# The S5 tail and the mLSTM branch of a two-block transformer kernel, put into one program block: the mLSTM in eight half-head units on six PSUM banks, S5's activation, gate and projection beside it

## What is computed

```python
h_ml = mlstm_memory(mq, mk, mv, mi + ml_i_b, mf + ml_f_b)      # 4 heads, keys of 64, values of 128
y_ml = jax.nn.sigmoid(mo) * h_ml.reshape(bsz, t, -1)
y_s5 = jax.nn.gelu(s5_ssm(su, ...))                            # 512 channels
y_s5 = y_s5 * jax.nn.sigmoid(y_s5 @ s5_glu_w + s5_glu_b)
gates = jax.nn.sigmoid(zg + branch_gate_b).reshape(bsz, t, N_BRANCH, D_MODEL)
merged = (gates[:, :, 0] * (y_gla @ proj_gla)
          + gates[:, :, 1] * (y_ml @ proj_ml)
          + gates[:, :, 2] * (y_s5 @ proj_s5))
```

```python
scores = (q @ k.T) * exp(d_intra - m)                # inside the chunk, causal
num = w_inter * (q @ mem) + scores @ v               # mem: the state from the chunks before
den = w_inter * (q @ norm) + sum(scores)
h = num / maximum(abs(den), exp(-m))
```

## Time and profile before

| | |
|---|---|
| median of 3 runs | 3596.35 us (3596.18 to 3603.19) |
| profiled execution, its own time | 3594.54 us |
| its span in the profile | 3592.8 us |
| PE busy | 3126.1 us (87%), 14192 matmuls |
| PEld / DVE / ACT / POOL busy | 2351.6 / 1329.7 / 958.9 / 814.7 us |

### The profile page before, as it was taken

How to read it: one execution, slowest core, us unless ns; L and a number is a source line. 1 busy time by engine, 2 the same in 40 slices (tenths; PEclk the granted TensorE clock), 3 DMA queues, 4 the chain that set the end, 5 groups by cost and what they waited for, 6 DMA issues and landing times. The chain is left out here.

```text
span 3592.8 us, 34192 instructions
## 1 busy us (share of the span) xinstructions
PE 3126.1 (87%) x14192; PEld 2351.6 (65%) x14192; DVE 1329.7 (37%) x1276; ACT 958.9 (27%) x1232; POOL 814.7 (23%) x381
## 2 busy tenths in 40 slices
PE   7599999989955778899999999996799999898587
PEld 3377777867744466688887877774466666676455
DVE  1453113263314343300001354204565653547265
ACT  0233212222131123311111443322233331445212
POOL 1133112243321012322222454321121111232100
PEclk9799999989977789899999999997899999899788
DMA  8211111431115042111111243121100001110201
GB/s 302 80 48 71 42 64 59 152 109 68 60 59 187 24 170 65 53 47 47 47 47 42 95 138 114 53 88 41 59 18 12 13 18 71 65 64 30 100 12 47
DMA packets 73557, 258.80 MB, mean 72 GB/s; under 512 B 7792, under 2 KB 12032, under 8 KB 72144
## 3 DMA queue, kind: packets, MB, share of 16 engines
q1 hardware_dynamic: 73424, 256.91, 20.4%
HBM read 206.52 MB, written 50.36 MB: 72 GB/s over the span
## 5 line engine op out<-in xcount | busy, mean ns | idle before, releaser
L277 POOL TENSOR_TENSOR w_lo_sb<-raw_w_sb,w_hi_sb 128x1024 fp32r<-128x1024 f32 x231 | 577.3, 2500 | 2083.3 <-ACT w_hi_sb L268 2083.3
L268 ACT ACTIVATE w_hi_sb<-raw_w_sb 128x1024 fp32r<-128x1024 f32 x231 | 243.2, 1053 | 479.7 <-PE ps L285 448.0
L285 PE MATMUL ps<-merged_parts_hi_sb,w_hi_sb 128*128 128x512 f32 x832 | 333.6, 401 | 22.5 <-PEq L698 12.1
L285 PE MATMUL ps<-merged_parts_lo_sb,w_hi_sb 128*128 128x512 f32 x832 | 332.6, 400 | 0.0
L285 PE MATMUL ps<-h_hi_sb,w_hi_sb 128*128 128x512 f32 x720 | 294.7, 409 | 27.7 <-PEq L1070 20.8
L285 PE MATMUL ps<-h_lo_sb,w_hi_sb 128*128 128x512 f32 x720 | 287.1, 399 | 0.0
L285 PE MATMUL ps<-merged_parts_hi_sb,w_lo_sb 128*128 128x512 f32 x832 | 275.3, 399 | 0.0
L285 PE MATMUL ps<-h_hi_sb,w_lo_sb 128*128 128x512 f32 x720 | 244.3, 399 | 0.0
L285 PE MATMUL ps<-z_lo,w_hi_sb 128*128 128x512 f32 x512 | 206.7, 404 | 0.0
L285 PEld LDWEIGHTS ps<-merged_parts_hi_sb,w_hi_sb 128*128 128x128 f32 x832 | 158.1, 190 | 68.6 <-issue 18.6
L2597 DVE TENSOR_TENSOR ffn_hidden_sb<-ffn_hidden_sb,ps 128x1024 f32 x20 | 24.4, 1221 | 431.6 <-PE ps L285 431.6
(11 more groups left out here) (563 smaller groups left out, 5725.0 us busy)
## 6 DMA issues: line engine op xcount, KB each, us to landing
raw_w_sb<-in_w SPq DMA_DIRECT2D x231, 512.0 KB, 3.2
ada_w_sb<-in_ada SPq DMA_DIRECT2D x48, 512.0 KB, 4.6
inbox_sb<-gates_out SPq DMA_DIRECT2D x24, 512.0 KB, 4.3
gates_out<-outbox_sb SPq DMA_DIRECT2D x16, 512.0 KB, 2.6
inbox_sb<-sums_out SPq DMA_DIRECT2D x16, 512.0 KB, 5.0
spilled_sum<-x_sb SPq DMA_DIRECT2D x32, 256.0 KB, 2.0
x_sb<-spilled_sum SPq DMA_DIRECT2D x2, 4096.0 KB, 13.7
x_sb<-in_x SPq DMA_DIRECT2D x1, 4096.0 KB
```

What stands on the lines that cost most here:

```text
L268: nc.scalar.activation(w_hi[:, n % RING].rearrange("p t m -> p (t m)"), raw_w[:, n % RAW], ACT.Copy).then_inc(w_rounded.sem, 1)
L277: nc.gpsimd.tensor_tensor(w_lo[:, n % RING].rearrange("p t m -> p (t m)"), raw_w[:, n % RAW], flat_hi, ALU.subtract).then_inc(w_split.sem, 1)
L285: mm = nc.tensor.matmul(o, wt, xs, start=start and part == 0 and xs is x_hi, stop=stop and part == 1)
```

## The change

Everything from the gelu to the mLSTM's last product becomes one `side_by_side` block with five parts: `activation()` (gelu and the first split), `glu` (a `dense` on banks 6 and 7, by halves of the tokens), `gated()` (the product and the second split, by halves), `memory()` (the mLSTM) and `merging` (merge_part number 1 on banks 6 and 7, by halves). The mLSTM has banks 0 to 5 and runs in eight units, four heads for the first 512 tokens and then four for the others; each half has its own reciprocal. The multiplication with the output gate moves to POOL, in front of the division, and the gate is loaded into S5's buffer. Loads are started at the block's beginning, from SP's one queue. The second block splits the mLSTM's result beside its projection. The empty block after S5 is gone. The diff's core (lines of semaphores and of allocation left out):

```diff
-        with nc.Block() as block:
-            @block.scalar
-            def _(act):
-                for t in range(4):
-                    nc.scalar.activation(by_block(Y[:, t]), by_step(u_[:, t]), ACT.Gelu_apprx_tanh)
-            split_block(4, lambda t: Y[:, t], YP)
-                linear(4, 4, moving(YP), ["act"] * 4, act_to(lambda m: glu[:, m], ACT.Sigmoid,
-                                                             bias=lambda m: V("glu_b", m)))
-                split_block(4, lambda t: Y[:, t], YP, mul=lambda t: glu[:, t])
-            side_by_side(merge_part(0.0, 1, 2, YP, scope, outbox, PAIRS))
-            outbox.emptied()
+            units = [(t, h) for t in range(2) for h in heads]
+            U = lambda n: 44.0 + 10.5 * n
+            INV = lambda t: U(4 * t + 3) + 13.0 - t
+            def activation():
+                def on_act(act, link):
+                    for t in range(4):
+                        yield 0.5 + 3.0 * t
+                        nc.scalar.activation(by_block(Y[:, t]), by_step(u_[:, t]), ACT.Gelu_apprx_tanh).then_inc(gelu_s.sem, 1)
+                        act.wait_ge(*gelu_s.at(t + 1))
+                        nc.scalar.activation(YP[0][:, t], Y[:, t], ACT.Copy).then_inc(hi_s.sem, 1)
...
+            glu = dense(7.0, 4, 4, moving(YP), ["act"] * 4, emit, (6, 7), 1.5, None, EARLY_HALVES, there)
+            def gated():
...
+                            yield end(u, h) + 1.2
+                            dve.wait_ge(free["act"].sem, glu.freed_half[(u, h)])
+                            nc.vector.tensor_tensor(Y[:, u, tokens(h)], Y[:, u, tokens(h)], sig[:, u], ALU.mult
+                                                    ).then_inc(gated_s.sem, 1)
...
+            def memory():
+                def on_sp(sp):
+                    yield -20.0
+                    for dst, row in ((G, 0), (lf, 1)):
+                        sp.dma_start(dst[:], rows_out[row]).then_inc(row_in.sem, 16)
...
+                    sp.dma_start(qk[:], ml_qk_out).then_inc(qk_in.sem, 16)
...
+                    yield 14.0
...
+                    sp.dma_start(og_[:], ml_og_out).then_inc(og_in.sem, 16)
...
+                    def weighing():
+                        for n, (t, h) in enumerate(units):
+                            a_ = h // 2
+                            yield U(n)
+                            if n == 0:
+                                pe.wait_ge(*rows_m.at(1))
+                                pe.wait_ge(*qa_s.at(2))
+                                pe.wait_ge(*states_s.at(2))
+                            else:
+                                pe.wait_ge(*arg_s.at(n))
+                            mm = nc.tensor.matmul(ps[:, 0], selx[:, h * P:(h + 1) * P], rx[:, tokens(t)], start=True,
+                                                  stop=True)
...
+                            yield U(n) + 6.5
+                            pe.wait_ge(*pr_s.at(n + 1))
+                            if n >= 2:
+                                pe.wait_ge(*num_s.at(n - 1))
...
+                    for n, (t, h) in enumerate(units):
+                        yield U(n) + 11.2
+                        if n == 0:
+                            pool.wait_ge(*og_in.at(16))
+                        pool.wait_ge(*num_s.at(n + 1))
+                        nc.gpsimd.tensor_tensor(Y[:, h, tokens(t)], Y[:, h, tokens(t)], og_[:, h, tokens(t)], ALU.mult
+                                                ).then_inc(og_s.sem, 1)
...
+                    yield from ordered(weights(), inverse(0), inverse(1))
+            two = [(u, (h,)) for h in range(2) for u in range(2)] + [(u, (h,)) for u in range(2, 8) for h in range(2)]
+            merging = merge_part(42.0, 1, 2, YP, scope, outbox, (6, 7), 2.3, None, two, gated_there)
+            side_by_side(activation(), glu, gated(), memory(), merging)
...
-            side_by_side(merge_part(0.0, 2, 1, YP, scope, None, PAIRS, 1.0, MP))
+            side_by_side(parts_of_y(), merge_part(0.0, 2, 1, YP, scope, None, PAIRS, 1.0, MP, None, parts_there))
```

More of the change, by code:

```diff
@@ L1266, in merge_part @@
             part = dense(at, 8, 4, moving(parts), ["dve"] * 8, emit, banks, pace,
-                         None if split_to else (outbox, lambda m: sums_out[n][:, m]))
+                         None if split_to else (outbox, lambda m: sums_out[n][:, m]), jobs, needs)
             to_memory = part.sp
@@ L2128, in build @@
[L2128 to L2142 removed]
+        Y = sb_in(y_scope, "y", [P, 4, T], high=True)
@@ L2406, in build, with parts_of_y, on_act, rest @@
         with ExitStack() as scope:
-            YP = split_in(scope, "y_parts", 4)
-            with ExitStack() as s2:
-                og = sb_in(s2, "ml_gate", [P, 4, T])
-                begin([(loaded, og[:], ml_og_out)])
-                finish(loaded)
-                split_block(4, lambda t: Y[:, t], YP, mul=lambda t: og[:, t])
-            side_by_side(merge_part(0.0, 2, 1, YP, scope, None, PAIRS, 1.0, MP))
+            hi_s, lo_dve, lo_pool = sem_again("ml_hi"), sem_again("ml_lo_dve"), sem_again("ml_lo_pool")
+            def parts_of_y():
+                def on_act(act, link):
+                    for t in range(4):
+                        yield -8.0 + 1.1 * t
+                        nc.scalar.activation(YP[0][:, t], Y[:, t], ACT.Copy).then_inc(hi_s.sem, 1)
+                def rest(eng, vec_eng, first, count):
+                    for t in (first, first + 2):
+                        yield -6.8 + 1.1 * t
+                        eng.wait_ge(*hi_s.at(t + 1))
+                        vec_eng.tensor_tensor(YP[1][:, t], Y[:, t], YP[0][:, t].bitcast(F32), ALU.subtract
+                                              ).then_inc(count.sem, 1)
+                return Part(None, None, on_act, lambda dve, link: rest(dve, nc.vector, 0, lo_dve),
+                            lambda pool, link: rest(pool, nc.gpsimd, 1, lo_pool))
+            def parts_there(k, h):
+                return [hi_s.at(k + 1), (lo_dve, lo_pool)[k % 2].at(k // 2 + 1)]
+            side_by_side(parts_of_y(), merge_part(0.0, 2, 1, YP, scope, None, PAIRS, 1.0, MP, None, parts_there))
+            over([(hi_s, 4), (lo_dve, 2), (lo_pool, 2)])
         y_scope.close()
```

561 lines of the change are left out of this document (316 added, 245 removed).

## The result

The changed kernel takes 3508.24 us (median of 4 runs, 3494.93 to 3513.29); before, in the same comparison, 3596.26 us (4 runs, 3586.34 to 3603.19). The ratio is 0.9752, with a 95% interval of 0.9716 to 0.9787: faster by 88 us. The prediction was 3503 us.

What follows compares the result with a forecast made beforehand. PE standing still or running slowly was taken as the bound. Summed: 54.2 to unit 0, 84.7 work, 6.5 stalls, 12.3 tail, 2.0 + 3.5 on top, a block of 163.2 us; gain 91.8, so 3503 us, range 3486 to 3530.

Steps and rivals of the forecast that it cites:

- rival 5: Merge output tiles: waits for the inbox hold up the units, slower than before; 3623 us at 15 us per tile; chance 0.02.
- Rival 4: Units: PE's clock stays at 1.2 GHz, 84.7 us of work become at most 169; 3587 us; chance 0.03.
- case 1: New block: PE-bound units behind a DVE-bound first part; 3503 us, own range 3492 to 3516; chance 0.58.
- rival 2: Queues hold each other up: units 13 to 14 us, first part 60; 3530 us, half of it 3517; chance 0.20.
- the rows' chain: First part: DVE's operations over the rows, behind Exp and Ln, take 9.75 us and end at 31.9.
- Unit 0 starts at 54.2: First part: from the gelu's table load to unit 0, including 21.3 us of DVE's list and 1 us for waits.
- Work 84.7 + stalls 6.5: Units: 46.8 heads, 36.5 projection, 1.4 spreadings, plus stalls including 3.4 at unit 4; last denominator ends at 145.4 us.
- 3.3 + 5.5 - 4.0: Unit 4: unit chain plus reciprocal chain minus PE's other work; PE waits 4.0 us or so, less overlapped merging, 3.4.
- The 0.234 us per matmul: Projection beside the units: matmul time from sigmoid spacing, 5.61 us for 24; 156 matmuls make 36.5 us.
- The tail 12.3: Block's end: second reciprocal 5.5, a spreading 0.4, four products 2.8, merging pairs 3.6; PE's last 30 matmuls lie beside it.
- On top 2.0 + 3.5: Whole block: 2.0 us for DVE slowed beside POOL in the first part, 3.5 us for slow matmuls after PE's pauses.
- The 3507 to 3517 us: Table loads: the total if each switch adds a drain of about 1.38 us, 2.66 in all, by the Trainium skill.

Runs made afterwards that it cites:

- e2b: Changed kernel with five added matmuls, results unread, ahead of unit 4's wait for its product; 3495.35 us in one execution.
- e1: Changed kernel with the first half's reciprocal chain issued on DVE behind unit 4's product instead of ahead of it; median 3505.33 us, ratio to before 0.9773.
- e12: Changed kernel with only three added matmuls at the block's end, around the second reciprocal's first spreading; 3519.58 us in one execution.
- e3: Changed kernel with the first merge taken out into a block of its own behind the units; median 3560.51 us, ratio to before 0.9919.
- e9: Changed kernel with the first merge in its own block and two added matmuls per unit, six in unit 4; 3517.87 us in one execution.
- e4: Changed kernel with the split of the mLSTM's result back in its own block ahead of the second merge; 3514.19 us in one execution.
- e0: The changed kernel run once more, unedited, beside the combined edits; median 3501.33 us of 6 runs, ratio to before 0.9779.

## Why the prediction was near, and where it was wrong

**Right.** Nearly all that the change brings is PE's standing time put beside other work (77.4 of the 81.3 us), and no wait for the inbox took its place: rival 5 fell, as did 4. The queues held each other up more than case 1 had it and less than rival 2: the first part took 58.9 us against rival 2's 60, but six of the seven steps were 10.1 to 13.3 us and not 13 to 14, and the gain up to the second merge, 74.55 us, lies between case 1's 91.8 and rival 2's 65. The last rounding (13.2 against 13.1), POOL's rest (15.7 against 16.0), Ln (22.2), the rows' chain (32.0 against 31.9), the stores' wait (3.4) and the way from there to the second merge's first product (10.4 against 10.8) stand as worked out.

**"Unit 0 starts at 54.2", with 2.0 on top for POOL.** 58.9 us. Two terms were mis-sized. DVE beside POOL cost 4.1 us in three operations, 2.1 of them in the one product that is held up only in the late executions. And I had put the half clock only behind PE's pauses just before unit 0 and at unit 4; it also lay over the states' matmuls, on the path in this execution, for some 2.5 us: from the last product ahead of the states to the first spreading it took 8.3 us, in e2b 5.8. Together the two are more than what is missing, so some smaller terms of the sum were too large.

**"Work 84.7 + stalls 6.5".** 103.65 us. The stall at unit 4 was 5.3 and not 3.4, for two reasons: the conversion in the reciprocal's chain took 1.73 us beside POOL, where the sum had 0.35, and the sum has a slip, since 3.3 + 5.5 - 4.0 is 4.8 and not 4.0. Behind the stall came slow matmuls: 36 of them took 12.1 instead of 7.6 us. e1 removes both and leaves 94.2 us, of which PE stands for only 0.65. So the other stalls, 3.1 us in the sum, didn't come, and the work itself was some 9 us too low. Most of that, 7.4 us, is the projection: its 156 matmuls took 43.9 us in e1, where the sum has 36.5. The 0.234 us per matmul holds inside a run of them; cut into groups of 3 to 9 between the units' own, 21 took 5.60 us in unit 6 of the changed kernel, 0.267 each, and in unit 0 of e1 the clock was low for 3.4 us besides.

**"The tail 12.3".** 18.6 us. 2.7 are the half clock over the last spreadings (e12). For the other 3.6 I have only the timeline: "PE's last 30 matmuls lie beside it", but twelve of them stand between the spreadings in PE's queue, so that DVE's products wait for spreadings behind them, and the last addition took 1.91 us beside POOL's slot rest. No run parts these two.

**"On top 2.0 + 3.5".** The 3.5 us for slow matmuls was, beside the work of the units, the term most in error. The clock cost about 2.5 us before unit 0, 4.5 at unit 4 and 2.7 in the tail, nearly 10 in all. I took the clock as a small addition, where it ought to have been asked at each stand of PE.

**What I had not seen at all** is why the merge pays beside the units. I counted its matmuls as filling idle time. e3 and e9 show that more than half of its worth (27.0 of 48.3 us) is that it keeps PE at 2.4 GHz through the units' chain. And this one part is most of the change: from the gelu's table load to the second merge's first product the kernel before takes 269.2 us, e3 243.5 and the changed kernel 194.9, so that 25.7 us of the gain are had without the merge beside the units, some 6 of them by the split (e4). Rival 4 (clock low through the units, chance 0.03) is what happens when the merge isn't there.

**The table loads.** The loads took 1.28 us, and the next activation started 0.02 us behind (1027.31 after 1026.01 + 1.28). The Trainium skill, page "ScalarE: Activation LUTs", section "What ACT_TABLE_LOAD costs", has a drain of 1.38 us for every switch; this trace doesn't agree for a load that follows a running queue, and the measurement decides. The 3507 to 3517 us of that rule hold the measured total, for another reason.

**The port.** Which of two operations is held up depends on the order of their starts: in the changed kernel POOL's slot rest began at 1048.49, DVE's product 0.22 us later took 2.76 us; in e2b the two began within 0.01 us of each other, DVE's took 0.69 and POOL's 2.94, and in e0, as close, it was DVE's that took 2.92. That is what the Trainium skill says on the page "SBUF — State Buffer", section "SBUF: two separate sides" (whoever starts first holds the shared port pair for the whole instruction), and the trace agrees. I had weighed it for operations with two SBUF inputs only; the conversions L2459 and L2515, with one, were held up too (1.65 against 0.68, 1.73 against 0.41). The page counts operations in a two-port performance mode too; whether these are such no run here shows.

## What to carry to other kernels

When you cost a stand of PE, add what follows it: here a stand of 5.3 us took another 4.5 us in slow matmuls, and the cure was to move 7 us of DVE work by one place in its queue. When independent matmuls can be laid between the links of a latency-bound chain, their worth can be more than the idle time that they fill, because the chain itself runs at the clock that they keep up; look at the granted clock of the chain alone. When you time a projection's matmuls, take them from a place where they are cut up as they will be. Read effects of a few us from a part of the trace between two events, and look at several executions before you call a start "late": the same instructions began up to 4.4 us apart.

## What the runs showed of the hardware

- Units of the mLSTM alone ran for 35 us and more at clock 0.50 while PE was busy for 30.5 of 34.9 us by its modelled times (e3). Two added matmuls of 0.87 us per unit raised it to 1.00 within the first two units, and the steps of units 2 and 3 fell from 11.6 to 7.8 us (e9).
- A DVE product and a POOL subtraction that start within 0.01 us of each other take 0.69 and 2.94 us or 2.92 and 2.37 us, by which of them is first (e2b, e0). In nine profiles of the same first part, the first spreading came at 55.1 to 55.9 us with the one order and at 58.9 to 59.5 with the other; the granted clock differed as well.
- The 2300 us behind the block varied by 20 us between profiles, with a mean granted clock of 0.930 to 0.932 where they were short and 0.923 to 0.926 where they were long.
- A 128x512 matmul of the type of v and the weights of the units stands in the trace as two instructions and takes 0.87 us at full clock, against 0.23 us for the rounded parts of the projections.
